# Differential and dilated attention units of a hybrid layer step: value products two units behind the scores, and where the gate's projection and the decode softmax stand

## What is computed

```python
(qa, ka, va, fa, ga), (qb, kb, vb), dil = _split_projection(_rmsnorm(h, norm_mix), w_in, lower_bounds)
oa, sa = _hgrn2_chunked(qa, ka, va, fa, s0)          # gated linear recurrence, 6 heads
ob = _diff_prompt(qb, kb, vb, lam)                   # (softmax1 - lam * softmax2) V, 6 heads
for g, (win, rate) in enumerate(((128, 1), (512, 4), (2048, 16))):
    o, lse = _dilated_prompt(qc, kc, vc, rate, win // rate)   # 4 heads, strided window
mix = concat(rmsnorm(oa) * silu(ga), rmsnorm(ob) * (1 - lam_init), combine(outs, lses))
h = h + mix @ w_out
h = h + _hier_moe(_rmsnorm(h, norm_ffn), ...)        # 16 experts, top 2
h = h + sigmoid(_rmsnorm(h) @ ple_w_gate) * (p @ ple_w_proj)
```

## Time and profile before

| | us |
|---|---|
| median of 3 runs | 1111.41 (1109.57 to 1111.67) |
| the profiled execution, its own time | 1112.19 |
| its span in the trace | 1110.4 |
| PE busy | 1044.8 (94% of the span) |
| DVE, ACT, POOL busy | 370.2, 249.1, 91.9 |
| mean granted clock of PE | 0.951 of full speed |

### The profile page before, as it was taken

How to read it: one execution, slowest core, us unless ns; L and a number is a source line. 1 busy time by engine, 2 the same in 40 slices (tenths; PEclk the granted TensorE clock), 3 DMA queues, 4 the chain that set the end, 5 groups by cost and what they waited for, 6 DMA issues and landing times.

```text
span 1110.4 us, 11245 instructions
## 1 busy us (share of the span) xinstructions
PE 1044.8 (94%) x4083; PEld 542.9 (49%) x4083; DVE 370.2 (33%) x766; ACT 249.1 (22%) x577; POOL 91.9 (8%) x113
## 2 busy tenths in 40 slices
PE   6998999999998999889899969999999999998996
PEld 3444555544465675555544544444444444443342
DVE  5017536533126566354531341111111110100443
ACT  3043222211222332432321110000000100011354
POOL 1000000000005460010010010000000000001200
PEclk9999999988999999875899969999999999999999
DMA  6735303313356542535353285689998999896301
GB/s 199 284 133 161 133 7 127 133 53 113 133 180 233 162 157 78 184 113 160 103 191 136 66 328 194 228 310 337 350 347 306 343 349 339 287 333 248 128 21 57
DMA packets 97099, 214.92 MB, mean 194 GB/s; under 512 B 14481, under 2 KB 42996, under 8 KB 96668
## 3 DMA queue, kind: packets, MB, share of 16 engines
q1 hardware_dynamic: 86288, 185.78, 47.9%
q0 software_dynamic: 5616, 19.89, 5.0%
q10 hardware_dynamic: 5148, 8.63, 2.0%
HBM read 191.97 MB, written 41.14 MB: 210 GB/s over the span
## 4 chain that ended last, share of the span: by engine, by line
PE 83%; DVE 7%; ACT 3%; DMA 3%; issue 2%; SPq 2%; POOL 1%; ACTq 0%; DVEq 0%; POOLq 0%
PE ps L1966 15%; PE ps L2389 10%; PE ps L2419 10%; PE ps L2395 10%; PE ps L1971 7%; PE ps L2484 5%; PE ps L2288 5%; PE ps L2258 2%; PE ps L2002 2%; PE ps L1974 2%; PE ps L2129 1%; PE ps L2048 1%; PE ps L2075 1%; PE ps L2207 1%; PE ps L2093 1%
## 5 line engine op out<-in xcount | busy, mean ns | idle before, releaser
L1966 PE MATMUL ps<-xT,EXPERT 128*128 128x512 f32 x384 | 182.2, 617 | 1.5 <-DVE EXPERT L1297 1.5
L1971 PE MATMUL ps<-EXPERT,xT 128*128 128x384 f32 (+1 forms) x384 | 118.7, 451 | 0.0
L2389 PE MATMUL ps<-EXPERT,aF 128*128 128x512 f32 x256 | 115.6, 605 | 1.3 <-DVE aF L1855 1.3
L2419 PE MATMUL ps<-EXPERT,dF 128*128 128x512 f32 x256 | 112.6, 592 | 1.6 <-ACT dF L1170 1.6
L2395 PE MATMUL ps<-EXPERT,aF 128*128 128x512 f32 x256 | 112.5, 592 | 0.0
L1966 PEld LDWEIGHTS ps<-xT,EXPERT 128*128 128x128 f32 x384 | 70.7, 195 | 80.8 <-issue 77.6
L1971 PEld LDWEIGHTS ps<-EXPERT,xT 128*128 128x128 f32 x384 | 77.7, 236 | 25.5 <-issue 3.6
L2389 PEld LDWEIGHTS ps<-EXPERT,aF 128*128 128x128 f32 x256 | 49.7, 194 | 64.4 <-issue 62.7
L2419 PEld LDWEIGHTS ps<-EXPERT,dF 128*128 128x128 f32 x256 | 48.6, 190 | 62.6 <-issue 60.7
L2395 PEld LDWEIGHTS ps<-EXPERT,aF 128*128 128x128 f32 x256 | 47.4, 190 | 53.6 <-issue 53.6
L2484 PE MATMUL ps<-EXPERT 128*128 128x512 f32 x128 | 57.7, 609 | 2.7 <-DVE EXPERT L1912 2.7
(11 more groups left out here) (429 smaller groups left out, 1181.6 us busy)
## 6 DMA issues: line engine op xcount, KB each, us to landing
EXPERT<-in_moe_w_gate SPq DMA_DIRECT2D x16, 2048.0 KB, 15.1
EXPERT<-in_moe_w_up SPq DMA_DIRECT2D x16, 2048.0 KB, 20.0
EXPERT<-in_moe_w_down SPq DMA_DIRECT2D x16, 2048.0 KB, 10.0
EXPERT<-in_w_in SPq DMA_DIRECT2D x13, 1536.0 KB, 6.7
out_win_sample<-in_cache_win SPq DMA_DIRECT2D x16, 1022.0 KB
Yd<-wk ACTq DMA_DIRECT2D x16, 512.0 KB, 8.4
aF<-in_cache_k_diff SPq DMA_DIRECT2D x32, 192.0 KB, 2.4
aF<-in_cache_v_diff SPq DMA_DIRECT2D x32, 192.0 KB, 2.4
```

The source lines that it names most:

```text
L1966: last = t.matmul(ps[:, u % 2, :], W_[:, c, c0:c0 + w], xT[:, c, 0:SEQ], start=(c == 0), stop=(c == DC - 1))
L1971: last = t.matmul(ps[:, u % 2, 0:w], rows_, W_[:, c, c0:c0 + w], start=(c == 0), stop=(c == DC - 1))
L2389: last = t.matmul(ps[:, 2 + 2 * b, :], xgT[b][:, c, :], wg_[b][:, c, :], start=(c == 0), stop=(c == DC - 1))
L2419: last = t.matmul(ps[:, 6 + hf, :], hT[b][:, c, :], wd_[b][:, c, hf * 512:(hf + 1) * 512], start=(c == 0), stop=(c == FC - 1))
```

## The change

1. `d_t` is now two units behind `d_s`, `d_pv` three; the same for `c_t` and `c_pv`. For this there are three probability buffers: `dP` cuts `wk` in three, `cP` takes three pieces of 512 of it. ACT waits for the transpose of unit n - 3 instead of n - 2 before it writes.
2. DVE takes the maximum of unit n before it weighs unit n - 1, where it did these the other way round.
3. `D_SHARE` 1.7 becomes 1.55. The rest of slab 3 (15 pieces) now stands in the dilated stage, `C_SHARE` = 2 pieces after each step. The partial sums of samples get an own buffer (`spart`).
4. Decode: the first `dec_q` comes 16 steps after `q_out` (11 before), then one every 4 (5). `dec_soft` moves from the dilated stage into the end of the differential one, right behind `dec_new`, and uses banks 2 and 3. `dec_norm` comes after `c_s(1)`. `gate_fn`, `gate_mul` and the four `ro` are tied to `dec_v` numbers 1, 3, 5, 8, 11 and 14.
5. The four early `krows` have a buffer each, so ACT waits for no store before them. The dilated results lie in the freed slab; so `w_out` comes in 3 parts and, after the results are stored (`w_more`), 2 parts.

```diff
-D_SHARE = 1.7
+D_SHARE = 1.55
+C_SHARE = 2
-Q_LAG, Q_EVERY = 11, 5
+Q_LAG, Q_EVERY = 16, 4
-RO_EVERY = 10
...
-        if 1 <= n <= nd:
-            d.append(("d_t", n - 1))
-        if n >= 2:
-            d.append(("d_pv", n - 2))
+        if 2 <= n < nd + 2:
+            d.append(("d_t", n - 2))
+        if n >= 3:
+            d.append(("d_pv", n - 3))
...
+    side = [("krows", u) for u in range(KR_EARLY)] + [("dec_wt",)] + [("dec_v", u) for u in range(2 * NS)]
+    beside = {("dec_v", 1): ("gate_fn",), ("dec_v", 3): ("gate_mul",)}
+    beside.update({("dec_v", 5 + 3 * i): ("ro", i) for i in range(NT)})
...
+        if st == ("d_t", nd - 2):
+            steps += [("dec_q", b) for _, b in keys] + [("cached", b + 2 - NS, 1) for _, b in keys]
+            keys = []
+            steps.append(("dec_soft",))
...
+    for k, st in enumerate(c):
+        steps.append(st)
+        if k == 1:
+            steps.append(("dec_norm",))
+        if st == ("c_pv", 2 * NT):
+            steps.append(("w_more",))
+        if todo:
+            for _ in range(min(C_SHARE, len(todo))):
+                project_one()
+            if not todo:
+                steps.append(("outputs",))
+                free = k + 1
+        elif side and k >= free:
+            free = k + C_PACE.get(beside_units(), 1)
...
+        dP = [wrow[:, k * 2 * SEQ:(k + 1) * 2 * SEQ] for k in range(3)]
+        cP = [wk[:, 0, 0:SEQ], wk[:, 1, 0:SEQ], wk[:, 0, SEQ:2 * SEQ]]
...
+        resid = EXPERT[:, DC * SLAB:DC * SLAB + NT * CW].rearrange("p (r n) -> p r n", r=NT)
...
+            def w_more():
+                sp.wait_ge(S_["res_st"], 16 * NT)
...
             def d_s(n):
-                if n:
-                    weigh(n - 1)
                 K = (n // HB + 1) * P
...
+                if n:
+                    weigh(n - 1)
...
             def dec_soft():
                 pe.wait_ge(S_["kused"], NS)
                 pe.wait_ge(S_["dec_row"], 1)
-                pe.wait_ge(S_["unit_ok"], NU)
+                pe.wait_ge(S_["d_exp"], NT * HB - 1)
```

More of the change, by code:

```diff
@@ L189, in schedule @@
     d = []
-    for n in range(nd + 2):
+    for n in range(nd + 3):
         if n < nd:
             d.append(("d_s", n))
-        if 1 <= n <= nd:
-            d.append(("d_t", n - 1))
-        if n >= 2:
-            d.append(("d_pv", n - 2))
+        if 2 <= n < nd + 2:
+            d.append(("d_t", n - 2))
+        if n >= 3:
+            d.append(("d_pv", n - 3))
     c = []
     nc_ = 4 * NT
-    for n in range(nc_ + 2):
+    for n in range(nc_ + 3):
         if n < nc_:
             c.append(("c_s", n))
[L202 to L205, removed]
+        if 2 <= n < nc_ + 2:
+            c.append(("c_t", n - 2))
+        if n >= 3:
+            c.append(("c_pv", n - 3))
     n_kr = len(key_row_units())
-    side = [("dec_soft",), ("krows", 0), ("dec_norm",)] + [("krows", u) for u in range(1, KR_EARLY)] + [("dec_wt",)]
-    side += [("dec_v", u) for u in range(2 * NS)]
+    side = [("krows", u) for u in range(KR_EARLY)] + [("dec_wt",)] + [("dec_v", u) for u in range(2 * NS)]
+    beside = {("dec_v", 1): ("gate_fn",), ("dec_v", 3): ("gate_mul",)}
+    beside.update({("dec_v", 5 + 3 * i): ("ro", i) for i in range(NT)})
     keys, at_q = [("dec_q", b) for b in range(NS)], None
@@ L227, in schedule, with beside_units @@
             at_q = k + Q_EVERY
-        if fresh and (not todo or todo[0][0] > summed[12]):
+        if fresh and todo[0][0] > summed[12]:
             fresh = False
             steps.append(("dec_new",))
[L231 to L257, removed]
+        if st == ("d_t", nd - 2):
+            steps += [("dec_q", b) for _, b in keys] + [("cached", b + 2 - NS, 1) for _, b in keys]
+            keys = []
+            steps.append(("dec_soft",))
+    assert not fresh and todo
+    def beside_units():
+        kind = side.pop(0)
         steps.append(kind)
@@ L260, in schedule @@
             steps.append(("cached", kind[1] // 2 + 2, 1))
+        if kind in beside:
+            steps.append(beside.pop(kind))
+        return kind[0]
+    free = 0
+    for k, st in enumerate(c):
[12 more added lines that the diff above has]
+            free = k + C_PACE.get(beside_units(), 1)
+    while side:
+        beside_units()
     steps.append(("dec_out",))
-    steps += [("ro", i) for i in range(n_ro, NT)]
     late = [("krows", u) for u in range(KR_EARLY, n_kr)]
@@ L661, in outputs @@
                             out(rows_, cvT[:, g, i])
-            does = dict(slab=load_slab, copy=copy, state_in=state_in, state_out=state_out, q_out=q_out, cached=cached,
+            def w_more():
+                sp.wait_ge(S_["res_st"], 16 * NT)
+                wo = a["w_out"][0].rearrange("(c p) n -> p c n", p=P)
+                sp.dma_start(EXPERT[:, WO_FIRST * D:WO_NOW * D].rearrange("p (c n) -> p c n", c=WO_NOW - WO_FIRST),
+                             wo[:, WO_FIRST:WO_NOW]).then_inc(S_["woload"], 16)
+            does = dict(w_more=w_more, slab=load_slab, copy=copy, state_in=state_in, state_out=state_out, q_out=q_out, cached=cached,
                         outputs=outputs)
@@ L794, in krows @@
                 i, groups = KU[u]
[L795 removed]
+                stage = kst[u]
                 pool.wait_ge(S_["kr_ok"], u + 1)
```

79 lines of the change are left out of this document (42 added, 37 removed).

## The result

The changed kernel takes 1117.83 us (median of 20 runs, 1111.01 to 1124.2) against 1111.26 for the kernel before (20 runs): a ratio of 1.0059, 95% interval 1.004 to 1.0078. It is slower by 6.6 us, where the sum forecast 1110.7, no change, and the chances leaned to faster (0.42). (The title names the distance of before: in the changed kernel the transposes stand two units behind the scores and the value products three.)

A forecast was written before the change was run, and what follows sets the result against it. PE, busy 94% of the span, was taken as the bound, losing about 36 us to waits and low clock in the dilated stage. Terms -5.6 + 7.0 + 3.3 + 3.1 - 9.6 + 1.1 = -0.7 gave 1110.7 us, range 1100 to 1120.

The forecast's parts named there:

- Part 1: Differential stage: greater distance and DVE's maximum before the weighing remove the waits of `d_t` for DVE, -5.6 us.
- Part 2: End of differential stage: PE's transpose in `dec_soft` waits openly for `dec_new` on DVE, +7.0 us.
- Part 3: Differential stage: with `dec_q` every 4 steps the key buffers come late and `d_t(22)` waits, +3.3 us, bounds 0 and 5.
- Part 4: Behind the wait at `dec_soft`: PE's next dense group runs at lower clock, +3.1 us, ends 0 and 4.
- the 3 to 7 us named as the sign: Sign that the forecast is right: half clock for 3 to 7 us behind the wait at `dec_soft`.
- Part 5: First part of dilated stage: gate pieces bring full clock, 3.2 us of waits left, -9.6 us, ends -12.8 and -5.
- Part 6: `gate_fn` behind `dec_v(1)`: 4.4 us of ACT, done before PE's next awaited copy, 0, at most 1 us.
- Part 8: `w_more`, later `outputs`: one more issue on SP, which is free then, 0, at most 1 us.
- Part 7: Rest of dilated stage: waits for values, merges and copies, half clock from `c_pv(10)`, +1.1 us, ends -5 and +4.
- the clock did not hold: Rival denied here: the clock holds through the dilated stage, about 1103 us, chance 0.34.
- the slow rival: Clock falls already between `krows(0)` and `dec_v(1)` in the dilated stage's first part, 1117 us, chance 0.22.
- the third rival: The distance of two units does nothing where PE is thin; dilated stage stays as long, 1118.5 us, chance 0.08.

The follow-up runs named there:

- lag_one_weigh_first: Changed kernel with the distances of before and DVE's order of before (weighing ahead of the next maximum): 1126.07 us, ratio 1.0143, 4 runs.
- soft_late: Changed kernel with `dec_soft` behind `d_pv(23)` instead of right behind `dec_new`: 1109.26 us, ratio 0.9972.
- ro_behind: Changed kernel with `ro(1)` to `ro(3)` right behind the merges, at `dec_v` 9, 12 and 15: 1116.25 us, ratio 1.0039.
- values_once: Changed kernel without loads of cached values after samples 0 and 1, decode outputs not computed: 1113.17 us, ratio 1.0014.
- soft_stores_ro_early: soft_late and stores_late together, with the four `ro` moved to `dec_v` 4, 5, 7 and 10: 1093.43 us, ratio 0.9855.
- stores_late: Changed kernel with the stores of rows moved behind the last loads of `w_out`: 1115.51 us, ratio 1.0017.
- ro_early: Changed kernel with only the four `ro` moved to `dec_v` 4, 5, 7 and 10: 1109.07 us, ratio 0.9976.
- stores_ro_early: stores_late and ro_early together, `dec_soft` left where the change has it: 1105.04 us, ratio 0.9951.
- gate_early: soft_stores_ro_early with `gate_fn` at `dec_wt` instead of `dec_v(1)`: 1097.17 us, ratio 0.9878.
- before_again: The kernel before, unchanged, run once more for a second profile: 1105.85 us, one run.

## Why the prediction was wrong

- **Part 1, distance: right.** The waits of the earlier trace rows at `d_t` are gone (5.6 us). The one of 2.4 in the second profile belongs to part 3. lag_one_weigh_first puts the distance at 9.3 us in this list.
- **Part 2, `dec_soft` (+7.0): right.** 6.94 us, and soft_late takes it away.
- **Part 3, key loop (+3.3): right.** 2.5 us at `d_t(22)`. DVE stood for POOL at `dec_q(4)`, (6) and (7), as forecast, 6.63, 0.61 and 1.84 us. In the second profile it stood 9.31 at `dec_q(4)`, the weighing behind that came late, and PE waited 2.4 at a `d_t` besides 1.8 at `d_t(22)`, 4.2 together. Of the ten profiles of kernels with the greater distance besides the first, eight have such waits for DVE, 1.9 to 3.1 us in all; so the first profile is a favourable one in this.

```profile
386.81 1.75 DVE L1557 TENSOR_REDUCE EXPERT<-aF 128x48 f32<-128x1536 f32 x1 [6.63 <-POOL EXPERT L801]
```
```profile
394.68 1.75 DVE L1557 TENSOR_REDUCE EXPERT<-aF 128x48 f32<-128x1536 f32 x1 [9.31 <-POOL EXPERT L801]
```

- **Part 4, clock behind it (+3.1): right.** 8.40 us with 8.32 busy at a mean clock of 0.54:

```profile
433.10:441.50 8.40, 8.32 (x34) 0.54 0.00 0
441.50:449.10 7.60, 7.60 (x35) 1.00 0.01 2
```

  At the factor of the earlier trace rows that is 0.92 x 8.32 x 0.43 = 3.3. Parts 2 and 4 together are 10.2, and soft_late measured 9.7. The stretch is longer than the 3 to 7 us named as the sign; its cost fits.
- **Part 5, first part of the dilated stage (-9.6): right.** 2.1 us of waits at clock 1.00, so 2.1 - 12.8 = -10.7.
- **Part 6, `gate_fn` (0, at most 1): within its bound as a wait, its effect on the clock open.** ACT's copy came 0.98 us late behind it. In the first profile of the changed kernel the clock fell at that wait (1.09 us for the four transposes behind it), in the second it did not (0.63); of the variants, ro_behind, values_once and soft_stores_ro_early show a fall there, and soft_late, stores_late, ro_early and stores_ro_early none. gate_early takes the wait away and is not faster, but has another in its place. So no loss by `gate_fn` is shown.
- **Part 8, `outputs` later (0): wrong.** This is the first step that failed. "SP is free then" looked at `w_more` alone. The 18 stores of rows hold SP for 14.9 us where they now stand (to 487.9); before, they were over at 468.2, long ahead of the loads of sample 2 at 486.73. Now they end 2.3 us after that buffer came free. stores_late: 4.7 us, where 0 to 1 was allowed, with intervals that just meet.
- **Part 7, rest of the dilated stage (+1.1): wrong, the term that carries the miss.** Parts 1 to 5 as measured sum to -5.6 + 6.9 + 2.5 + 3.3 - 10.7 = -3.6, and the first product of the output projection came 3.6 later in the first profile, so the rest is +7.2, which holds the loss of part 8 too. (In the second profile it is more: there the stretch is 6.7 longer than before.) My sum had 18.5 of waits and 6 of clock; measured are 14.2 of waits, and the remaining 16.4 (23.4 + 7.2 - 14.2) are clock. Counted directly, 34.3 busy us at half clock, times 0.43, are 14.7. I let full clock last until `c_pv(10)`, while it fell ahead of `dec_v(4)`, and again behind each of the next two groups of waits (busy time of PE in the three stretches, below). The places of the `ro` were named rightly, their price was not: the forecast had 10.9 us of waits at the three merges and 6 of clock behind the first. The measured waits there are only 4.3, none at `c_pv(10)`, 0.78 at `c_pv(12)` and 3.53 at `c_pv(14)`, where 4 or more was the sign; PE came late to them, at half clock. Still, moving the `ro` gives 9.2. What this part of the sum had wrong is therefore the clock: how early it falls, and that waits and clock stand in for each other, so that what is gained in one is partly lost in the other (before and before_again).

```profile
492.20:509.00 16.80, 13.69 (x58) 0.50 0.53 154
...
520.60:533.00 12.40, 12.31 (x53) 0.50 0.52 172
...
541.20:553.00 11.80, 8.27 (x39) 0.50 0.01 1
```

The rivals: the clock did not hold. It did not fall in the first part either, so that the slow rival's 1117 lies near the measured 1117.83 is luck. So is the third rival's 1118.5: the distance did something (9.3 us), and the first part of the stage did gain. Its sum is off as well, since it adds 7.8 to the forecast of 1110.7, not to the 1111.41 of before. Two smaller slips, 3.2 for 1.7 + 1.4 in part 5 and 18.5 for the 18.4 of part 7, change nothing.

The Trainium skill's page "TensorE: Matmul & The Clock Gate", section "A second HAM failure mode: psum-queue depth-cycling", was cited for a loss of clock without long waits. The traces agree in part: stretches of over 10 us at half clock hold almost no idle time. But in the changed kernel each began behind a recorded wait, and in ro_early the same thin work ran at 1.00 from 535.3 to 553.2, once the waits of 0.78 and 1.52 us ahead of it were gone and the one at `c_pv(14)` was 1.00. The other three kernels with the early `ro` show the same full clock at that place, so here taking waits away did bring clock back. It does not do so everywhere: the same wait is followed by half clock in one profile and not in another (part 6).

**What stays open.** soft_stores_ro_early still has stretches at half clock:

```profile
482.50:498.50 16.00, 15.59 (x72) 0.58 0.53 159
498.50:505.50 7.00, 5.09 (x38) 1.00 0.92 247
505.50:517.00 11.50, 10.77 (x50) 0.53 0.64 215
```

They begin behind waits of 0.98 and 0.38, and of 1.86 us. Why waits of 0.9 and 1.2 us at 472 and 479 cost no clock in the changed kernel, and did in gate_early and stores_ro_early, no run here tells; nor what a faster read-back of the strided results, which holds the first merge, would be worth. Nor was a version tried in which the changed list keeps the pieces of the gate for this stretch.

## What to carry to other kernels

When a step moves in a list that all engines walk, price it on every queue: here 15 us of stores on SP slid in front of the loads of the next buffer, and small operations of DVE in front of the merges that PE waits for. A greater distance between producer and consumer pays (9.3 us here), but it and the order on the engine between them belong together: the new order with the old distance cost 33 us. And where a stage is thin, look at a wait and at the half clock behind it together, then ask what PE will wait for next when it comes earlier. Moving the `ro` took away 6.6 us of waits and a stretch of half clock and was worth 9.2; but in before_again 10.7 us of clock bought only 2.5, and leaving out most loads of values only 5.0, since the merges and their DMA came next.

## What was not expected of the hardware

- The last 550 us, where PE's work is the same in all kernels, took between 548.6 and 555.2 us from profile to profile, and the first 264 between 261.0 and 266.9. Between the two profiles of the changed kernel it is 2.5 us, nearly all of it at one place: ahead of the last gate PE waited 1.96 instead of 0.64 us, and the first 16 products behind took 9.97 instead of 8.80.
- The same 18 stores held SP for 11.4 us before, 14.9 in the changed kernel and 9.2 in stores_late, at a DMA share of 0.90, 0.90 and 0.97 in these stretches: the time to issue a store is not a constant of its size.
- One kernel can run one stage at different clocks: 0.72 and 0.83 in two profiles of the kernel before, over 102.9 and 100.4 us. And the same wait of 0.98 us, at the same place of the list, was followed by half clock in four of the nine profiles that have it.
